# Value stages: an earlier first row sum, a block's weight split by halves, and the x transfers issued by ScalarE

## The chip, the cores and the metric

The kernel runs on one core of a Trainium2 chip. Times are device microseconds of one execution. A core has five engines that run their own instruction streams and wait for one another through semaphores: TensorE (PE) multiplies matrices, VectorE (DVE) and ScalarE (ACT) work elementwise on SBUF and PSUM, GpSimd (POOL) elementwise on SBUF, and SyncE (SP) issues transfers. ScalarE can issue transfers too.

## The reference

```python
def mixer_a(h, w_in, ln_g, ln_b, w_s, b_s, w_out):
    u, v, z = jnp.split(h @ w_in, 3, axis=-1)          # h: 2048 x 1024, w_in: 1024 x 6144
    u = jax.nn.gelu(u)
    v = layer_norm(jax.nn.gelu(v), ln_g, ln_b)
    ... # causal 128 x 128 mixing of v in each chunk of 128 positions, 8 channel groups
    y = u * mixed.reshape(B, S, A_WIDTH) * jax.nn.silu(z)
    return y @ w_out                                   # 2048 x 1024

# layer A
h = rms_norm(x, a_norm[i]) * (1.0 + scale) + shift
x = x + gate * mixer_a(h, ...)
# layer B: the shared k, v are projected from rms_norm(x, kv_norm); sliding-window attention
# over the same x, an output gate, an output projection; then one final rms_norm
```

All inputs are float32: x is 1 x 2048 x 1024.

## The kernel before, in words

**Token groups.** Layer A is worked through in four groups of 512 tokens (`NG = 4`, `i` = 0 to 3). A group has a value stage (v of `w_in`), eight steps for u and z with the spatial mixing, and the out projection with `w_out`. Layer B follows for all tokens.

**Precision by splitting.** Every product is three matmuls (`split3`, lines 2361 to 2363): each operand is a rounded part and a rest, hi x hi, hi x lo and lo x hi. For raw weights ScalarE rounds (`hi`, line 1364) and GpSimd subtracts to get the rest (`lo`, line 1130; for the out blocks (2,q) VectorE does, line 2116). Weight pieces come by halves: half of a unit is 512 KB raw. Some weight combinations are kept in DRAM already split ("kept": 1 MB for half of a unit) and need no rounding.

**Value stage, groups 1 to 3.** The product is done with seven block products instead of eight (a Strassen-like scheme), twice: `v_blocks(0)`, then `v_blocks(1)`. Units are numbered `v_unit(i, 0..13)`; unit n < 7 is block n of the first half. Blocks 0, 3 and 5 (units 0, 3, 5, 7, 10, 12) have raw weights, the others kept ones. Blocks 2, 4, 5 and 6 multiply sums of h (`s1` to `s4`), which GpSimd forms in the first value half (`s_sums`, `s_add`), ScalarE rounds (`s_round`) and GpSimd completes (`s_rest`, line 1176). They serve for both halves. The sum buffer `hfw` shares its place with `uu`, so VectorE waits for all eight sums of a group before it writes the third block's output.

**Out projection.** Again seven block products, (m, q) for product m and half q of the rows, in the order (0,0) (1,0) (0,1) (1,1) (2,0) (2,1) (3,0) (3,1) ... (6,1). The left operands `yb` are rounded by ScalarE (`factor_round`, line 1540) and completed by VectorE (`factor_rest`, line 2093). `out_keep(m)` (line 1547) copies a finished product out of PSUM on ScalarE. Meanwhile the next group's x is loaded (`load_x`), squared (`x_squares`), scaled (`x_scale`) and transposed during the last blocks.

**Order of transfers.** All weight loads are issued by SP in one hand-written order, each half when TensorE has freed its buffer. Between them stand the stores of x1 (group i-1's residual, `x1d`, line 993, after unit 9, four transfers of 512 KB) and `load_x(i + 1)` (line 928, one transfer of 2 MB, after out block (2,0)'s load). SP's transfers go on the queue that the profile calls q1, ScalarE's on q10.

Of the kernel before, what the change touches and what calls it, by code (L numbers as in the profile page):

```python
# [12 lines left out]
P = 128  # L13
# [4 lines left out]
T = 512  # L18
NG = SEQ // T
# [257 lines left out]
def combs_out(i, m):  # L277

    return 16 * sum(comb_stores(comb) for comb in COMBS if comb[0] <= i and comb[4] == m)
# [115 lines left out]
def yoco_kernel(nc, x, c, positions, a_norm, a_ada_w, a_ada_b, a_w_in, a_ln_g, a_ln_b, a_w_s, a_b_s,  # L395
# [3 lines left out]
    with ctx:  # L399
# [181 lines left out]
        def at(name, i, k):  # L581

            return per[name] * i + k
# [70 lines left out]
        def pieces(u, k):  # L654

            return PIECES_BY[u] + k
# [120 lines left out]
        def _(sp):  # L777
# [141 lines left out]
                    else:  # L919
                        b_half(u, hh)  # L920

            def load_x(n):
                if n >= 1:
                    sp.wait_ge(xt_full, at("xt_full", n - 1, 8))
                    sp.wait_ge(v_gelu, at("v_gelu", n - 1, 16))
                    sp.wait_ge(comb_out[0], combs_out(0, 0))
                    sp.wait_ge(piece_done, pieces(ao_block(n - 1, 1, 0), 4))
                sp.dma_start(xs[:], x[0, T * n:T * n + T, :].rearrange("(c p) d -> p c d", p=P)).then_inc(x_in, 16)

            def load_residual(i):  # L930
                if i == NG - 1:
                    sp.wait_ge(xt_full, at("xt_full", i, 8))
# [40 lines left out]

            for n in range(2 * KT):
                if n == 5:
                    load_x(0)
                load_ada(n)
            unit(0)
            unit(1)
# [1 line left out]
            for i in range(NG):  # L981
                if i == 0:
                    for j in range(4):
                        a_stage(0, j)
                else:
                    for n in range(2, V_UNITS[i]):
                        unit(v_unit(i, n))
                        if n == 11:
                            load_split(split_at(i, 3))
                        if n == 9:  # L990
                            sp.wait_ge(ao_read, at("ao_read", i - 1, 8))
                            for cnk in range(NC):
                                sp.dma_start(x1d[i - 1, :, cnk], x1[:, cnk, :]).then_inc(x1_out, 16)
                for g in range(GROUPS + 1):
                    a_stage(i, 4 + g)
                    if i >= 1 and g >= 2:
                        keep_turned(i - 1, g - 2)
                for n in range(2, 16):
                    if i == 0 and n == 15:
                        combs_kept(0)  # L1000
                    unit(ao_first(i) + n)
                    if i >= 1 and n == 4:
                        keep_turned(i - 1, GROUPS - 1)
                    if i < NG - 1 and n == 4:
                        load_x(i + 1)
                    if n == 7:
                        load_residual(i)
                    if i == NG - 1 and n in (6, 8, 10):
                        load_xk(0, n // 2 - 3)
                    if i == NG - 1 and n == 14:  # L1010

                        sp.wait_ge(piece_done, pieces(ao_block(i, 5, 1), 4))
                        sp.dma_start(hb0[:].bitcast(F32), hbd[0, 0:4].rearrange("k p a t -> p k a t")) \
                            .then_inc(hb0_in, 16)
# [78 lines left out]
        def _(pool):  # L1093
# [75 lines left out]
                pool.drain()  # L1169
                s_add(2, q, h_block(0, 1, q), ALU.subtract, s_whole(0, q))  # L1170

            def s_rest(i, s):
                for q in range(2):
                    there = S_ORDER[s][:, 2 * q:2 * q + 2]
                    pool.wait_ge(s_hi, s_parts(i, s, q))
                    g.tensor_tensor(there[:, :, 1, :], s_whole(s, q), there[:, :, 0, :].bitcast(F32),
                                    ALU.subtract).then_inc(s_lo, 1)
# [24 lines left out]
            for i in range(NG):  # L1202
# [5 lines left out]
                else:  # L1208

                    pool.wait_ge(piece_done, PIECES_BY[FIRST[i]])  # L1210
                    pool.wait_ge(xt_full, at("xt_full", i, 8))
                    s_sums(0)
                    pool.wait_ge(h_hi, at("h_hi", i, 8))
                    s_sums(1)
                    s_rest(i, 0)
                    for q in range(2):
                        s_add(3, q, h_block(0, 0, q), ALU.subtract, h_block(1, 0, q))
                    lo(v_unit(i, 3))
                    s_rest(i, 1)
                    s_rest(i, 2)  # L1220
                    lo(v_unit(i, 5))
# [128 lines left out]
        def _(act):  # L1350
# [46 lines left out]
            def load_positions(j):  # L1397
                act.dma_start(tabi[:], positions[:, T * j:T * j + T].broadcast_to([P, T])).then_inc(pos_in, 16)

            def squares(src, total, waste):  # L1400
                act.drain()
                return s_.activation(waste, src, ACT.Square, accum_out=total)
# [71 lines left out]
            for i in range(NG):  # L1474
# [20 lines left out]
                def v_blocks(sv):  # L1495
# [5 lines left out]
                        s_.activation(ut[:, c, :], bank(2 * sv + c), ACT.Copy).then_inc(first_kept, 1)  # L1501
                    if sv == 0:
                        s_round(i, 0, (1,))
                        s_round(i, 1)
                        s_round(i, 2)
                    hi(v_unit(i, 7 * sv + 3))
                    if sv == 0:
                        s_round(i, 3)
                    else:
                        x1_squares(i - 1)  # L1510
                    hi(v_unit(i, 7 * sv + 5))
                    for c in range(2):
# [88 lines left out]
                factor_round(2, 1)  # L1601
                hi(ao_block(i, 2, 1), (0,))
                out_keep(1)
                hi(ao_block(i, 2, 1), (1,))
                for q in range(2):
                    factor_round(3, q)
# [1172 lines left out]
```

## Time and profile before

| | |
|---|---|
| median of 3 runs | 2218.93 us (2217.34 to 2219.06) |
| profiled execution | 2219.44 us |
| its span, first to last instruction | 2217.7 us |
| mean granted TensorE clock | 0.996 |
| TensorE matmuls busy | 2150.9 us, 97% |
| VectorE, ScalarE, GpSimd busy | 65%, 49%, 54% |

The span is what the trace covers; the difference to the execution's own time lies outside the instructions. The granted clock is TensorE's clock as a share of full speed. In the rows below, a time in brackets is how long the engine sat idle before the instruction and what it waited for; "xN" merges N like instructions. A matmul's own duration of 0.39 us overlaps its neighbours'.

### The profile page before, as it was taken

The numbers are of one execution on the slowest core, as the hardware profiler recorded it, in microseconds if no ns is written. First come the engines' busy times: TensorE is split into PE (matmuls) and PEld (weight loads), VectorE is DVE, ScalarE is ACT, GpSimd is POOL, SyncE is SP. The second block draws the span as 40 slices with busy tenths as digits, with TensorE's granted clock in tenths as the row PEclk, the third lists the DMA queues.
The fourth block names the chain that finished last, engine by engine and source line by source line (L and its number), as shares of the span: only waits on it lengthen the run. The fifth ranks groups of instructions, "written<-read, shape, count | busy, mean of one in ns | idle before, by whom it ended". The sixth has DMA issues, their size and how long they took to land.

```text
span 2217.7 us, 29383 instructions
## 1 busy us (share of the span) xinstructions
PE 2150.9 (97%) x10410; PEld 1801.0 (81%) x10410; DVE 1440.5 (65%) x1761; ACT 1095.3 (49%) x2050; POOL 1195.1 (54%) x913
## 2 busy tenths in 40 slices
PE   5999999999999999999999999999999999999998
PEld 4887778788888878888777888887888888888887
DVE  6956548757486864554974673767767657656854
ACT  4334446634545744445653445534545646545653
POOL 3456675845553865544594645441535555454542
PEclk9999999999999999999999999999999999999999
DMA  9888889785558785557877556899686697887654
GB/s 347 307 306 308 312 315 356 231 308 174 196 198 324 285 315 191 200 179 269 314 259 283 181 181 218 323 348 365 244 297 225 253 359 266 280 309 288 206 205 171
DMA packets 244787, 592.89 MB, mean 267 GB/s; under 512 B 20929, under 2 KB 96801, under 8 KB 244257
## 3 DMA queue, kind: packets, MB, share of 16 engines
q1 hardware_dynamic: 241680, 585.71, 73.5%
q10 hardware_dynamic: 2960, 5.30, 0.7%
q8 instruction: 83, 1.36, 0.2%
q14 instruction: 64, 0.52, 0.1%
HBM read 461.96 MB, written 119.54 MB: 262 GB/s over the span
## 4 chain that ended last, share of the span: by engine, by line
PE 75%; DMA 6%; POOL 6%; DVE 5%; ACT 3%; DVEq 2%; POOLq 1%; issue 1%; SPq 1%; ACTq 0%
PE ps L2361 22%; PE ps L2363 22%; PE ps L2362 22%; DMA w_raw<-in_a_w_in 3%; POOL w_lo L1130 3%; PE ps L2566 2%; PE ps L2615 1%; PE ps L2616 1%; POOL cbl L1149 1%; PE ps L2641 1%; DVE acc L1812 1%; ACT w_hi L1364 1%; DMA w_lo<-a_weights_combined 1%; PE ps L2650 1%; DVE yb L2093 1%
## 5 line engine op out<-in xcount | busy, mean ns | idle before, releaser
L1130 POOL TENSOR_TENSOR w_lo<-w_raw,w_hi 128x1024 fp32r<-128x1024 f32 x244 | 650.0, 2682 | 569.6 <-ACT w_hi L1364 569.4
L1364 ACT ACTIVATE w_hi<-w_raw 128x1024 fp32r<-128x1024 f32 x260 | 272.0, 1057 | 418.3 <-DMA w_raw<-in_a_w_in 372.7
L2361 PE MATMUL ps<-h,w_hi 128*128 128x512 f32 x1024 | 403.3, 394 | 9.7 <-POOL w_lo L1130 8.3
L2363 PE MATMUL ps<-h,w_lo 128*128 128x512 f32 x1024 | 398.9, 390 | 0.0
L2362 PE MATMUL ps<-h,w_hi 128*128 128x512 f32 x1024 | 398.7, 389 | 0.0
L2361 PEld LDWEIGHTS ps<-h,w_hi 128*128 128x128 f32 x1024 | 192.2, 188 | 55.3 <-POOL w_lo L1130 14.3
L2363 PEld LDWEIGHTS ps<-h,w_lo 128*128 128x128 f32 x1024 | 192.2, 188 | 40.7
L2362 PEld LDWEIGHTS ps<-h,w_hi 128*128 128x128 f32 x1024 | 192.4, 188 | 38.9 <-issue 0.2
L2361 PE MATMUL ps<-r,w_hi 128*128 128x512 f32 x480 | 191.6, 399 | 1.9 <-issue 1.9
L2363 PE MATMUL ps<-r,w_lo 128*128 128x512 f32 x480 | 187.7, 391 | 0.0
L2362 PE MATMUL ps<-r,w_hi 128*128 128x512 f32 x480 | 187.3, 390 | 0.0
L2361 PE MATMUL ps<-w_hi,yb 128*128 128x512 f32 x448 | 179.2, 400 | 7.1 <-DVE w_lo L2116 3.5
L2071 DVE SCALAR_TENSOR_TENSOR wz<-wz,ps 128x512 f32<-128x512 f32 x64 | 43.7, 686 | 210.5 <-ACT wz L1580 210.5
L2363 PE MATMUL ps<-w_hi,yb 128*128 128x512 f32 x448 | 175.8, 392 | 0.0
L2362 PE MATMUL ps<-w_lo,yb 128*128 128x512 f32 x448 | 175.6, 392 | 0.0
L2093 DVE TENSOR_TENSOR yb<-vy,yb 128x1024 fp32r<-128x1024 f32 x48 | 114.4, 2383 | 42.5 <-ACT yb L1540 39.2
L1269 POOL TENSOR_SCALAR_AFFINE_SELECT p_edge<-pt 64x256 fp32r<-64x256 f32 x64 | 27.1, 423 | 187.7 <-ACT pt L1735 186.5
L2361 PE MATMUL ps<-w_hi,r 128*128 128x512 f32 (+1 forms) x352 | 125.5, 357 | 2.7 <-DMA r<-kv_input 1.7
L1735 ACT ACTIVATE pt<-ps 128x512 fp32r<-128x512 f32 x64 | 38.4, 600 | 179.6 <-PE ps L2641 179.2
L2363 PE MATMUL ps<-w_hi,r 128*128 128x512 f32 (+1 forms) x352 | 123.6, 351 | 0.0
L2362 PE MATMUL ps<-w_lo,r 128*128 128x512 f32 (+1 forms) x352 | 123.5, 351 | 0.0
L2361 PE MATMUL ps<-w_hi,h 128*128 128x512 f32 x272 | 107.9, 397 | 4.5 <-POOL w_lo L1130 4.2
(277 smaller groups left out, 4902.6 us busy)
## 6 DMA issues: line engine op xcount, KB each, us to landing
w_raw<-in_a_w_in SPq DMA_DIRECT2D x256, 256.0 KB, 3.6
w_hi<-b_weights_split SPq DMA_DIRECT2D x104, 512.0 KB, 4.7
w_lo<-b_weights_split SPq DMA_DIRECT2D x104, 512.0 KB, 6.3
w_raw<-in_a_w_in SPq DMA_DIRECT2D x52, 512.0 KB, 4.7
w_raw<-in_a_w_out SPq DMA_DIRECT2D x48, 512.0 KB, 5.4
w_hi<-v_weights_combined SPq DMA_DIRECT2D x48, 512.0 KB, 3.9
w_lo<-v_weights_combined SPq DMA_DIRECT2D x48, 512.0 KB, 5.2
w_hi<-a_weights_combined SPq DMA_DIRECT2D x32, 512.0 KB, 6.6
```

Of the source, the lines that this page charges most:

```text
L1130: g.tensor_tensor(wlo[p][:, rows_], raw[p][:, rows_], whi[p][:, rows_].bitcast(F32), ALU.subtract).then_inc(w_lo, 1)
L1149: last = g.tensor_tensor(cbl[m][:, rows_], cbr[m][:, rows_], cbh[m][:, rows_].bitcast(F32), ALU.subtract)
L1269: return g.affine_select(out=heads, in_=in_, compare_op=ALU.is_ge, fill=0.0, base=0, pattern=[[0, 4], [1, HEAD]], channel_multiplier=-1)
L1364: s_.activation(whi[p][:, rows_], raw[p][:, rows_], ACT.Copy).then_inc(w_hi, 1)
L1735: s_.activation(pt[:, 0, :], bank(6), ACT.Copy).then_inc(pt_hi, 1)
L1812: v.scalar_tensor_tensor(there, rows_, sc[:, kt:kt + 1], there, ALU.mult, ALU.add).then_inc(ada_used, 1)
L2071: v.scalar_tensor_tensor(wz[:, ft, :], wz[:, ft, :], 1.0, bank(2 + ft), ALU.add, ALU.mult) \
L2093: v.tensor_tensor(there[:, :, 1, :], y_factor(m, q), there[:, :, 0, :].bitcast(F32), ALU.subtract) \
L2361: t_.matmul(dst_, stat[0], mov[0], start=start, stop=False)
L2362: t_.matmul(dst_, stat[0], mov[1], start=False, stop=False)
L2363: return t_.matmul(dst_, stat[1], mov[0], start=False, stop=stop)
L2566: last = t_.matmul(bank(4 + ft, P, P * cnk), vs[:, cnk, P * ft:P * ft + P], wst[:, g, :], start=True, stop=True)
```

## The change

Four edits. In GpSimd's stream the first row sum's rest for the first half is moved ahead of the second half's sums, and the fourth block's (unit 3's) weight rests are split around the two sums of the fourth kind. In ScalarE's stream the rounding of unit 3 is split around the second sum's rounding. The stores of x1 move from SP (after unit 9) to ScalarE (after unit 10's rounding, ahead of `x1_squares`). The loads of x for groups 1 to 3 move from SP to ScalarE, behind `out_keep(1)`; the load for group 0 stays with SP.

```diff
@@ block.sync
-            def load_x(n):
-                if n >= 1:
-                    sp.wait_ge(xt_full, at("xt_full", n - 1, 8))
-                    sp.wait_ge(v_gelu, at("v_gelu", n - 1, 16))
-                    sp.wait_ge(comb_out[0], combs_out(0, 0))
-                    sp.wait_ge(piece_done, pieces(ao_block(n - 1, 1, 0), 4))
-                sp.dma_start(xs[:], x[0, T * n:T * n + T, :].rearrange("(c p) d -> p c d", p=P)).then_inc(x_in, 16)
...
                 if n == 5:
-                    load_x(0)
+                    sp.dma_start(xs[:], x[0, 0:T, :].rearrange("(c p) d -> p c d", p=P)).then_inc(x_in, 16)
...
                         if n == 11:
                             load_split(split_at(i, 3))
-                        if n == 9:
-                            sp.wait_ge(ao_read, at("ao_read", i - 1, 8))
-                            for cnk in range(NC):
-                                sp.dma_start(x1d[i - 1, :, cnk], x1[:, cnk, :]).then_inc(x1_out, 16)
...
-                    if i < NG - 1 and n == 4:
-                        load_x(i + 1)
@@ block.gpsimd
-            def s_rest(i, s):
-                for q in range(2):
+            def s_rest(i, s, halves=(0, 1)):
+                for q in halves:
...
                     s_sums(0)
+                    s_rest(i, 0, (0,))
                     pool.wait_ge(h_hi, at("h_hi", i, 8))
                     s_sums(1)
-                    s_rest(i, 0)
+                    s_rest(i, 0, (1,))
+                    lo(v_unit(i, 3), (0,))
                     for q in range(2):
                         s_add(3, q, h_block(0, 0, q), ALU.subtract, h_block(1, 0, q))
-                    lo(v_unit(i, 3))
+                    lo(v_unit(i, 3), (1,))
                     s_rest(i, 1)
@@ block.scalar
+            def load_x(n):
+                act.wait_ge(xt_full, at("xt_full", n - 1, 8))
+                act.wait_ge(v_gelu, at("v_gelu", n - 1, 16))
+                act.wait_ge(comb_out[0], combs_out(0, 0))
+                act.wait_ge(piece_done, pieces(ao_block(n - 1, 1, 0), 4))
+                act.dma_start(xs[:], x[0, T * n:T * n + T, :].rearrange("(c p) d -> p c d", p=P)).then_inc(x_in, 16)
...
                     if sv == 0:
                         s_round(i, 0, (1,))
+                        hi(v_unit(i, 3), (0,))
                         s_round(i, 1)
+                        hi(v_unit(i, 3), (1,))
                         s_round(i, 2)
-                    hi(v_unit(i, 7 * sv + 3))
-                    if sv == 0:
                         s_round(i, 3)
                     else:
+                        hi(v_unit(i, 10))
+                        act.wait_ge(ao_read, at("ao_read", i - 1, 8))
+                        for cnk in range(NC):
+                            act.dma_start(x1d[i - 1, :, cnk], x1[:, cnk, :]).then_inc(x1_out, 16)
                         x1_squares(i - 1)
...
                 out_keep(1)
+                if i < NG - 1:
+                    load_x(i + 1)
                 hi(ao_block(i, 2, 1), (1,))
```

## Rows read from the trace of the kernel before

**Rows 1.** The page's list: busy time (share of the span) x instructions.

```profile
PE 2150.9 (97%) x10410; PEld 1801.0 (81%) x10410; DVE 1440.5 (65%) x1761; ACT 1095.3 (49%) x2050; POOL 1195.1 (54%) x913
```

**Rows 2.** TensorE in order of time, first value half, group 1: start, duration, instruction.

```profile
430.28 0.39 PE L2362 MATMUL ps<-w_lo,h 128*128 128x512 f32 x1
430.51 0.39 PE L2363 MATMUL ps<-w_hi,h 128*128 128x512 f32 x1
431.58 0.47 PE L2361 MATMUL ps<-w_hi,s 128*128 128x512 f32 x1 [0.68 <-issue]
...
437.65 0.50 PE L2361 MATMUL ps<-w_hi,h 128*128 128x512 f32 x1 [0.38 <-POOL w_lo L1130]
...
440.52 0.39 PE L2361 MATMUL ps<-w_hi,h 128*128 128x512 f32 x1
```

**Rows 3.** TensorE in order of time, unit 10 in groups 1, 2, 3.

```profile
477.33 0.50 PE L2361 MATMUL ps<-w_hi,h 128*128 128x512 f32 x1 [1.28 <-POOL w_lo L1130]
...
830.63 0.50 PE L2361 MATMUL ps<-w_hi,h 128*128 128x512 f32 x1 [0.84 <-POOL w_lo L1130]
...
1186.73 0.50 PE L2361 MATMUL ps<-w_hi,h 128*128 128x512 f32 x1 [0.95 <-POOL w_lo L1130]
```

**Rows 4.** TensorE in order of time, out block (2,1) of group 2.

```profile
1074.98 0.76 PE L2361 MATMUL ps<-w_hi,yb 128*128 128x512 f32 x1 [2.10 <-DVE w_lo L2116]
...
1078.43 0.39 PE L2363 MATMUL ps<-w_hi,yb 128*128 128x512 f32 x1
```

**Rows 5.** Windows view, that stretch: length, engines' busy time, PEclk, DMA share, GB/s.

```profile
1074.00:1080.00 6.00, 5.02 (x15) 4.08 (x16) 5.82 (x4) 6.00 (x7) 3.53 (x2) 0.72 0.99 365
```

**Rows 6.** GpSimd in order of time, first value half, group 1.

```profile
426.05 1.29 POOL L1159 TENSOR_TENSOR s1f<-hfw 128x512 f32<-128x512 f32 x1
...
430.19 2.54 POOL L1176 TENSOR_TENSOR s<-s2f,s 128x512 fp32r<-128x512 f32 x2
432.69 2.55 POOL L1159 TENSOR_TENSOR s3f<-hfw 128x512 f32<-128x512 f32 x2
435.19 4.78 POOL L1130 TENSOR_TENSOR w_lo<-w_raw,w_hi 128x1024 fp32r<-128x1024 f32 x2
```

**Rows 7.** SP in order of time, second value half, group 1.

```profile
460.60 2.86 SPq L993 DMA_DIRECT2D x_kept<-x  x4
463.50 2.62 SPq L807 DMA_DIRECT2D w_raw<-in_a_w_in  x2
```

**Rows 8.** ScalarE in order of time, unit 10's rounding, group 1.

```profile
473.76 1.06 ACT L1364 ACTIVATE w_hi<-w_raw 128x1024 fp32r<-128x1024 f32 x1 [7.96 <-DMA w_raw<-in_a_w_in]
```

**Rows 9.** SP in order of time, out projection, group 2.

```profile
1057.42 0.63 SPq L928 DMA_DIRECT2D xs<-in_x  x1
1059.32 3.04 SPq L797 DMA_DIRECT2D w_raw<-a_weights_combined  x2
```

**Rows 10.** ScalarE in order of time, out block (2,1), group 2.

```profile
1070.58 1.06 ACT L1364 ACTIVATE w_hi<-w_raw 128x1024 fp32r<-128x1024 f32 x1 [2.73 <-DMA w_raw<-a_weights_combined]
```

**Rows 11.** VectorE in order of time, the same place.

```profile
1072.23 1.47 DVE L1917 TENSOR_TENSOR up<-up,ps 128x512 f32<-128x512 f32 x2 [1.58 <-ACT uq L1547]
1073.62 2.35 DVE L2116 TENSOR_TENSOR w_lo<-w_raw,w_hi 128x1024 fp32r<-128x1024 f32 x2
```

**Rows 12.** Queues from 698 to 699 us: packets, MB, share of 16 engines.

```profile
q10 hardware_dynamic: 56, 0.22, 52.9%
q1 hardware_dynamic: 72, 0.16, 44.3%
```

**Rows 13.** SP in order of time, out blocks (3,0) and (3,1), group 1.

```profile
710.79 8.53 SPq L801 DMA_DIRECT2D w_raw<-in_a_w_out  x4
```

**Rows 14.** ScalarE in order of time, second half of block (3,1), group 1.

```profile
723.75 1.06 ACT L1364 ACTIVATE w_hi<-w_raw 128x1024 fp32r<-128x1024 f32 x1 [1.01 <-DMA w_raw<-in_a_w_out]
```

**Rows 15.** VectorE in order of time, rests of the fifth block's factor, group 1.

```profile
725.80 2.92 DVE L2093 TENSOR_TENSOR yb<-vy,yb 128x1024 fp32r<-128x1024 f32 x1 [0.43 <-ACT yb L1540]
...
731.92 2.50 DVE L2093 TENSOR_TENSOR yb<-vy,yb 128x1024 fp32r<-128x1024 f32 x1
```

**Rows 16.** TensorE in order of time, out block (5,1), group 1.

```profile
756.11 0.50 PE L2361 MATMUL ps<-w_hi,yb 128*128 128x512 f32 x1 [0.22 <-POOL w_lo L1130]
```

## Prediction

> **What bounds the kernel now.** I read the page's list of engines first: TensorE's matmuls fill 2150.9 of 2217.7 us [rows 1]. So an edit is worth what it gives back of TensorE's remaining pauses, or costs in new ones, and everything else waits behind it. Next came TensorE's rows in order of time, looking only at rows with an idle time in brackets. In a stretch without pauses matmuls start 0.227 us apart (430.28, 430.51) [rows 2]. At the pause behind them the step is 1.07, so 0.84 is lost where the bracket says 0.68: a loss is the bracket plus 0.16. From 437.65, behind a pause, twelve matmuls take 2.87 where twelve steps are 2.73, so about 0.14 more goes in restarting. I price a pause at its bracket plus 0.3. A unit of 24 matmuls is 5.46 us, its half 2.73.
>
> The pauses that the edits can reach are of three kinds; the first two come once in each of the token groups 1 to 3:
> - first value half: before the third and the fourth block, 0.68 and 0.38 [rows 2]; the other two groups repeat it to within 0.03;
> - second value half: before its fourth block (unit 10), 1.28, 0.84 and 0.95 [rows 3];
> - out projection of group 2: 2.10 before block (2,1), after which eight steps take 3.45 us instead of 1.82 [rows 4]; the granted clock of that stretch is 0.72, a mix of 2.4 and 1.2 GHz [rows 5].
>
> **First value half: the row sums.** The third block needs GpSimd's rest of the first row sum. Now both halves' sums are made first, the second from 426.05 to 430.19 (4.14 us), then the two rests (2.54), two sums of the fourth kind (2.55) and the fourth block's two weight rests (4.78) [rows 6]. With the first rest moved ahead: it runs 426.05 to 427.3, the sums to 431.5, the other rest to 432.7, the fourth block's first weight half to 435.1, the two sums to 437.6, the second weight half to 440.0. TensorE would begin the third block at 430.74 (no pause), want its second half at 433.5 (there since 432.7), begin the fourth at 436.2 (there since 435.1), and want that block's second half at 438.9. That is there at 440.0, because GpSimd has done the same work by then in either order. So the pause moves: this half began at 440.52 [rows 2] and will begin at about 440.05, plus the restart. Worth 0.4 us a group, 1.2 in three. Bounds: 0, if GpSimd runs 0.4 slower in the new order; 5.0 if both pauses went whole (0.98 + 0.68 with restarts, three times). I take 1.2, since every duration in it is from a row.
>
> ScalarE's reordered roundings (the fourth block's split among them) run about 1 us ahead of GpSimd and cost nothing. VectorE waits for all eight sums before the third block's output; those now end 2.5 us later, at 437.6 instead of 435.2. It takes up slack that VectorE has by the fifth block, so I price it at nothing; without that cover it would hold the banks of the fifth block and cost up to 1 us.
>
> **Second value half: the x stores.** SP issues four 512 KB stores of x1 at 460.60, takes 2.86 us over them, and only then issues unit 10's weights at 463.50 [rows 7]. ScalarE is free for them, waits 7.96 us and starts at 473.76 [rows 8]: 10.3 us from issue to use. Then GpSimd takes 2.4 and TensorE has paused. After the change SP issues that load when TensorE frees its buffer, eight halves after 440.52, at 462.3 (near 462 with the first pauses shorter). The 2 MB of stores are gone from ahead of it, 5.7 us at the 365 GB/s of a full stretch [rows 5], which leaves 4.6 of the 10.3, say 6. So ScalarE rounds near 468.5 and GpSimd is done by 472, where TensorE wants it at 475.9. The stores are issued by ScalarE when it has dispatched unit 10's rounding, near 471, and are under way until 479, beside units 11 and 12. Unit 12 is wanted at 486.8, two units later. The wait for `ao_read` holds nothing: the squares behind it wait for the same. ScalarE's issuing of four stores (2.9 us, SP's own time) lies in the wait that is gone. I count all three pauses: (1.28 + 0.84 + 0.95) + 3 x 0.3 = 4.0 us. Bounds: 0 and 4.0.
>
> The Trainium skill (DMA: Bandwidth & Descriptors, Rules for kernel authors) says that spreading transfers over SP and ScalarE brings no bandwidth, because all run on the same engines, and saves only issue time. By it this edit would give only what the stores' later place gives; were they in flight with unit 10 all the same, the 4.0 would be near 0.
>
> **Out projection: the x load, its gain.** In group 2, SP issues the 2 MB x load at 1057.42 and block (2,1)'s first half at 1059.32 behind it [rows 9]. ScalarE gets it at 1070.58, after a wait of 2.73 [rows 10], so its copy of `uq` and with it VectorE are late (a wait of 1.58); VectorE then adds for 1.4 us and needs half of 2.35 for the first weight rest [rows 11]. Without the wait VectorE starts its additions at 1070.7, has that rest at 1073.4, and TensorE, which wants it at 1072.7, pauses 0.5. Now the step costs 2.26 + 1.63 = 3.9 [rows 4]; after, 0.8, at full clock. Gain 3.1.
>
> **Out projection: the x load, its cost.** ScalarE issues it behind the copy of `uq`, two units (11 us) later than SP did. Where the two queues were both loaded, in one microsecond 56 packets of q10 (ScalarE's) and 72 of q1 (SP's) moved [rows 12]: about one for one. The x load is 512 packets of 4 KB (a row of 1024 floats); at 64 a microsecond it is under way for 8 us, and lands some 10 us after its issue, before the squares need it. But in these 8 us SP fetches block (3,1), packets of 2 KB (512 floats), 256 to a half: each half takes 4 us instead of 2. In group 1 the last of them is issued near 719 [rows 13] and ScalarE waits for it until 723.75 [rows 14]; I put it 2.3 later, at 726.0. The rounding behind it is what VectorE waits for at 725.80 [rows 15], and from there VectorE is busy without a gap up to the factors of block (5,1), where TensorE pauses 0.22 already [rows 16]. VectorE gets some back: its step of 2.50 at 731.92 [rows 15] runs beside GpSimd, and moved behind GpSimd's work takes 1.23 as half of 2.35 did [rows 11]. So 2.3 becomes 1.0 in group 1; the same reckoning gives 0.6 in group 0 and 1.0 in group 2. ScalarE and GpSimd also start block 3's rests 0.4 to 0.9 sooner, worth 0.3 in groups 0 and 1. In all: 3.1 - 1.0 - 1.0 - 0.6 + 0.6, say +0.8 (in group 2 I leave 0.3 for the small pauses that its big one covered). Bounds: +3.7 if VectorE feels nothing, -3.6 if it gets nothing back (3.1 less 1.9, 2.3 and 2.5).
>
> The Trainium skill (DMA: Bandwidth & Descriptors, Queues, rings and completion order) has each engine take turns between rings, packet by packet. By that rule 4 KB packets get twice the bytes of 2 KB ones, as reckoned, and the trace agrees (56 against 72).
>
> **Sum.** 1.2 + 4.0 + 0.8 = 6.0 us. The profiled execution took 2219.4 (1.7 of it outside its span, which no edit touches), which gives 2213.4; it stands 0.5 above the median of the three runs, 2218.93, so I predict 2212.9, 0.27% faster. A measurement of this kernel tells about 0.2%, 4.4 us.
>
> **The rivals.**
> - *The x load is free (or frees more).* VectorE's 2.3 us vanish in its overlap with GpSimd: sum 1.2 + 4.0 + 3.1 = 8.3, 2210.6. For it: VectorE's operations shrink from 2.5 to 1.2 beside an idle GpSimd. Against: no gap on VectorE in 30 us. 0.25.
> - *VectorE gives nothing back.* Out projection -3.6: sum 1.6, 2217.3, no change that can be measured. 0.15.
> - *A second queue is no second road.* By the skill's rule above, as a mechanism here: the stores, moved by ScalarE, still meet unit 10 and then units 11 and 12, and TensorE's pause moves to one of these. Gain of the stores' edit 0: 6.0 - 4.0 = 2.0, 2216.9. Against: unit 12 is wanted 7 us after the stores end. 0.1.
> - *Slower: the late x load throttles the clock.* TensorE's pause at block (5,1) reaches 2 us, as the one in group 2 did [rows 4], and the granted clock falls, 1.6 more each time. It decides from a delay of about 2 us on VectorE that isn't given back. In three groups: 1.9 + 2.3 + 2.5 and 3 x 1.6 = 11.5 lost, against 1.2 + 4.0 + 3.1 = 8.3: 3.2 slower, 2222.1. 0.1.
> - The row sums do nothing (their pause moves whole): 1.2 less, inside the forecast.
>
> **How the numbers follow.** Forecast 0.4, its own range 2211 to 2215.5; the free load 0.25, nothing back 0.15, no second road 0.1, slower 0.1. One thing is common to all: a clock that falls elsewhere by chance, 1.6 either way. From 2208.5 to 2219.0 lies all but the slow case and the far end of the free one, 8 in 10. Faster by over 0.2% means below 2214.5: all of the free case and 0.9 of the forecast, 0.62; slower 0.1; the rest, 0.28, within.
>
> **What would show it.** Right: no pause before unit 10; third block at its step, a pause of about 0.9 in the middle of the fourth; in group 2 a pause below 1 at (2,1) and clock 1.0; ScalarE's wait for block (3,1) in group 1 ending 2 us later, relative to TensorE, and a pause near 1.2 at (5,1). Wrong: a pause at units 11 to 13 or in the fifth block of the first half; a granted clock below 1 in groups 0 to 2; the x load landing more than 12 us after its issue.

## The result, and the profile after

The changed kernel takes 2223.78 us (median of 16 runs, 2220.62 to 2230.14); the kernel before takes 2218.64 beside it (16 runs, 2216.03 to 2221.58). The ratio is 1.0027, with a 95% interval of 1.0020 to 1.0034. That is 6.0 us slower (4.4 to 7.5; the two medians are 5.1 apart), where I had forecast 6.0 faster. The time lies outside my range, and on the side to which I gave 0.1. The profiled execution of the changed kernel was its slowest run, 2230.14 us, span 2228.3, so its trace shows more loss than a usual run. A second profile of the same kernel (c1 below, 2218.77 us) tells which of it returns.

From the page of the changed kernel, its list of engines (for [rows 1]):

```profile
PE 2153.1 (97%) x10410; PEld 1801.6 (81%) x10410; DVE 1448.6 (65%) x1761; ACT 1095.8 (49%) x2050; POOL 1184.5 (53%) x913
```

TensorE still sets the time, so the difference has to lie in its pauses. Its rows in order of time (start, duration, instruction, idle time and releaser), pauses only; the first three lie in the value stage of group 1 and answer to [rows 2, 3], the other three in the out projections of groups 1 and 2, the fifth of them in the place of [rows 4]:

```profile
442.14 0.50 PE L2362 MATMUL ps<-w_hi,h 128*128 128x512 f32 x1 [1.01 <-POOL w_lo L1116]
...
462.44 0.47 PE L2362 MATMUL ps<-w_hi,h 128*128 128x512 f32 x1 [0.95 <-DVE vy L1975]
...
490.44 0.50 PE L2362 MATMUL ps<-w_hi,s 128*128 128x512 f32 x1 [0.56 <-POOL w_lo L1116]
...
753.07 0.50 PE L2362 MATMUL ps<-w_hi,yb 128*128 128x512 f32 x1 [3.27 <-DVE yb L2094]
...
1081.19 0.47 PE L2362 MATMUL ps<-w_hi,yb 128*128 128x512 f32 x1 [0.60 <-DVE w_lo L2117]
...
1112.02 0.50 PE L2362 MATMUL ps<-w_hi,yb 128*128 128x512 f32 x1 [2.64 <-DVE yb L2094]
```

The first is the pause that I had moved to the middle of the fourth block. The second is new: the first block of the second value half waits for VectorE. The third stands before unit 12 (its operand is `s`), while unit 10 pauses no more; in groups 2 and 3 unit 12 pauses 0.75 and 1.72. The one of 0.60 stands before block (2,1) of group 2, where the kernel before had 2.10. The pauses of 3.27 and 2.64 stand before block (5,0). Behind the one at 753 the granted clock falls to 0.72, a mix of 1.2 and 2.4 GHz. The table of windows shows it (columns: the stretch, its length, then busy time and count of TensorE's matmuls, its weight loads, VectorE, ScalarE and GpSimd, then granted clock, DMA share, GB/s):

```profile
755.00:760.00 5.00, 5.00 (x17) 3.91 (x17) 4.82 (x3) 1.13 (x2) 5.00 (x3) 0.72 0.26 57
```

For all comparisons I cut each trace into stages by the starts of TensorE's first matmul in each stage. The table gives their durations in us. "Va" and "Vb" are the first and the second value half, each up to the next unit's start, in groups 1, 2, 3; "out" is the out projection of groups 0, 1, 2. The names are those of the experiments below:

| kernel | out 0 / 1 / 2 | Va 1 / 2 / 3 | Vb 1 / 2 / 3 |
|---|---|---|---|
| before | 81.31 / 82.08 / 84.08 | 39.82 / 39.81 / 39.83 | 39.66 / 39.23 / 39.33 |
| before, again (c2) | 81.29 / 82.51 / 82.79 | 39.80 / 39.82 / 40.59 | 40.16 / 38.89 / 38.21 |
| after | 82.59 / 86.24 / 86.06 | 40.63 / 40.60 / 40.60 | 39.31 / 39.21 / 40.21 |
| after, again (c1) | 82.72 / 82.86 / 82.64 | 39.46 / 40.59 / 39.45 | 39.17 / 39.86 / 38.93 |
| e1, sums only | 81.20 / 82.10 / 81.94 | 39.46 / 39.49 / 39.45 | 40.19 / 39.47 / 39.00 |
| e4, sums and two drains | 81.25 / 82.10 / 82.11 | 39.45 / 39.46 / 39.50 | 39.79 / 40.07 / 38.79 |
| e2, stores only | 81.28 / 82.08 / 82.11 | 39.81 / 39.81 / 40.59 | 39.68 / 41.46 / 39.67 |
| e3, load only | 82.85 / 84.36 / 82.62 | 39.80 / 40.57 / 39.80 | 39.64 / 38.17 / 39.12 |
| e7, load late on SP | 84.37 / 84.86 / 85.55 | 40.61 / 40.57 / 39.81 | 38.23 / 38.97 / 38.85 |
| e8, sums, stores on SP last | 81.46 / 82.17 / 82.08 | 40.57 / 40.59 / 40.60 | 39.33 / 39.69 / 40.26 |
| e9, stores late on SP | 81.34 / 82.08 / 82.17 | 40.59 / 39.79 / 39.80 | 42.51 / 41.65 / 42.27 |
| e10, stores split | 81.18 / 83.26 / 82.32 | 40.61 / 39.80 / 39.81 | 38.20 / 38.08 / 38.08 |
| e11, stores early | 81.44 / 81.97 / 81.84 | 39.81 / 40.28 / 40.27 | 38.08 / 38.17 / 38.20 |
| e12, e11 with sums | 81.36 / 82.08 / 82.30 | 40.60 / 40.60 / 40.63 | 38.20 / 38.18 / 38.20 |

A second value half without a pause is seven units, 7 x 5.46 = 38.2.

### The profile page after: what moved, and what is told of

Same layout as the page of the kernel before. It is cut to its first block, busy times and chain, and to the rows that moved or that the text cites. A ratio compares the mean times of both kernels' runs of the same rounds, so it can differ in the third digit from the quotient of the medians.

```text
span 2228.3 us, 29383 instructions
## 1 busy us (share of the span) xinstructions
PE 2153.1 (97%) x10410; PEld 1801.6 (81%) x10410; DVE 1448.6 (65%) x1761; ACT 1095.8 (49%) x2050; POOL 1184.5 (53%) x913
## 4 chain that ended last, share of the span: by engine, by line
PE 74%; DMA 6%; DVE 6%; POOL 6%; ACT 3%; DVEq 2%; POOLq 1%; issue 1%; SPq 1%; ACTq 0%
PE ps L2362 22%; PE ps L2364 22%; PE ps L2363 22%; DMA w_raw<-in_a_w_in 3%; POOL w_lo L1116 3%; PE ps L2567 2%; PE ps L2616 1%; PE ps L2617 1%; POOL cbl L1135 1%; PE ps L2642 1%; ACT w_hi L1352 1%; DVE acc L1813 1%; DVE yb L2094 1%; DMA w_raw<-in_a_w_out 1%; PE ps L2651 1%
## 5 line engine op out<-in xcount | busy, mean ns | idle before, releaser
L2362 PE MATMUL ps<-h,w_hi 128*128 128x512 f32 x1024 | 403.3, 394 | 10.1 <-POOL w_lo L1116 8.4
```

What stands on the lines that cost most here:

```text
L2362: t_.matmul(dst_, stat[0], mov[0], start=start, stop=False)
```

## The experiments

e1, e2, e3, e7, e9, e10 and e11 are the kernel before with one edit; e4, e8 and e12 have one more on top of e1's; c1 and c2 are the changed kernel and the kernel before once more. Each was timed beside the kernel before (median 2217.37 beside e1 to e4, 2217.25 beside e7, e8, e9 and c1, 2216.94 beside e10, e11, e12 and c2), in 11 or 12 runs, e7 and e9 in 5.

### The three edits, one by one

**e1: the row sums alone.**

```diff
                     s_sums(0)
+                    s_rest(i, 0, (0,))
                     pool.wait_ge(h_hi, at("h_hi", i, 8))
                     s_sums(1)
-                    s_rest(i, 0)
+                    s_rest(i, 0, (1,))
+                    lo(v_unit(i, 3), (0,))
                     for q in range(2):
                         s_add(3, q, h_block(0, 0, q), ALU.subtract, h_block(1, 0, q))
-                    lo(v_unit(i, 3))
+                    lo(v_unit(i, 3), (1,))
```

with ScalarE's roundings in the matching order.

> Only the order of the row sums, their rests and the fourth block's roundings in the first value half is changed; stores and x load stay on SP. Theory 'starved': in the changed kernel VectorE waits for all eight sums, its next 128x512 operation then starts inside an unbroken run of GpSimd and takes 8.09 us instead of 1.77, and TensorE pauses 0.95 at the first block of the second value half, three times: 3 x (0.95 + 0.3) = 3.75 lost against the 1.2 that I forecast as gain, so about 2.5 slower than before (2221.2), with the 8.09 and the 0.95 in its trace in all three groups. Rival 'sums are harmless' (the 8.09 comes from the queues' other order): 1.2 faster, 2217.4, and the operation near 1.8.

Measured: 2216.95 us, ratio 1.0000 (0.9991 to 1.0008). The operation took 0.89 us in group 1 and no long one stood in any group; the pause of 0.95 was absent. In its trace the first halves gain 0.36 us each, 1.1 in three, as forecast (1.2). The time itself can't show it: 1.1 lies within its interval of 2 us either way.

**e4: the same with gaps in GpSimd's stream.**

```diff
                     lo(v_unit(i, 5))
+                    pool.drain()
                     s_rest(i, 3)
+                    pool.drain()
                     lo(v_unit(i, 7))
```

> The row sums' order as in the changed kernel, and GpSimd drains before the rest of the fourth row sum and before unit 7's rest, which opens small gaps in its stream; nothing else is changed. Theory 'starved': a gap lets VectorE's operation through, it takes 2 to 4 us instead of 8, the pause of 0.95 goes, and the time is 2 to 3 below the kernel with the sums alone. Rival: the gaps are too short, the operation stays at 8.09 and the time at that of the sums alone; then only the operation's start, not GpSimd's breath, matters.

Measured: 2216.48 us, ratio 0.9997 (0.9988 to 1.0006), no long operation. Since e1 had none either, the gaps had nothing to cure: inconclusive.

**e2: the stores alone.**

```diff
-                        if n == 9:
-                            sp.wait_ge(ao_read, at("ao_read", i - 1, 8))
-                            for cnk in range(NC):
-                                sp.dma_start(x1d[i - 1, :, cnk], x1[:, cnk, :]).then_inc(x1_out, 16)
...
                     else:
+                        act.wait_ge(ao_read, at("ao_read", i - 1, 8))
+                        for cnk in range(NC):
+                            act.dma_start(x1d[i - 1, :, cnk], x1[:, cnk, :]).then_inc(x1_out, 16)
                         x1_squares(i - 1)
```

Unit 10's rounding stands just ahead of these lines, so ScalarE's order is that of the changed kernel.

> Only the stores of x1 move, from SP ahead of unit 10 to ScalarE behind unit 10's rounding. Theory of the prediction: the three pauses at unit 10 go, 4.0 faster (2214.6). Rival 'no second road' (the changed kernel's trace has 0.56, 0.54 and 1.72 before unit 12 where unit 10 had 1.28, 0.84 and 0.95): the pause moves to unit 12 and stays about as large, 0 to 1 faster (2217.6 to 2218.6).

Measured: 2221.02 us, ratio 1.0023 (1.0013 to 1.0033), slower. No pause at unit 10; before unit 12 the pauses are 1.31, 2.21 and 1.19. The rival's place is right, and even its 0 to 1 faster was too kind. The profile is of e2's slowest run, 2226.04 us.

**e3: the x load alone.**

```diff
-                    if i < NG - 1 and n == 4:
-                        load_x(i + 1)
...
                 out_keep(1)
+                if i < NG - 1:
+                    load_x(i + 1)
```

with `load_x` written for ScalarE as in the changed kernel.

> Only the x load moves, from SP to ScalarE behind the copy of uq. Theory 'late beside block (3,1)': the load takes the transfers' time from block (3,1), VectorE is late, and TensorE pauses 3.3 at (5,0) in group 1 and 2.6 in group 2 with the clock falling (1.6 each), against the 3.1 gained at (2,1) in group 2: some 4 slower than before (2222 to 2223). Rival of the prediction: 0.8 faster (2217.8), with pauses near 1.2 at block 5; then the large pauses of the changed kernel come from VectorE's phase that the other two edits set.

Measured: 2220.34 us, ratio 1.0017 (1.0009 to 1.0026), slower by 2 to 6. Its largest pauses in the out projections are 1.44 in group 0, 1.59 in group 1 (at 750.28) and 0.71 in group 2, all at (5,0) and near the 1.2 that I had forecast at block 5. The total is not near it, because there was next to no gain at (2,1) to set against them. The clock did not fall there.

### The same kernels once more

> The changed kernel once more, for a second profile. If its large pauses at (5,0) (3.27 and 2.64 us) and VectorE's operation of 8.09 us belong to it, they are there again in the same groups; if they are chance, groups 1 and 2 of the out projection take 84 and 82.6 us as with the x load alone moved, and 8.09 turns up in some groups only. Time 2220 to 2224.

Measured: 2222.41 us, ratio 1.0023 (1.0014 to 1.0032). The pauses at (5,0) are 1.33, 0.70 and 0.70, the clock stays at 1.00 behind them, and the long operation is there in group 2 alone. So 3.27 and 2.64 with the fallen clock belong to one execution, not to each.

> The kernel before once more, for a second profile. If the pause of 2.10 us at block (2,1) of group 2, on which I put a gain of 3.1, belongs to the x load's place, it is there again and the third out projection takes 84 us; if it was chance (no trace of the kernels that leave the x load on SP has it), it takes 82.1 and the pause is 0.6 to 0.9. Time 2217 to 2218, ratio 1.000.

Measured: 2217.75 us, ratio 1.0007 (0.9997 to 1.0017). At block (2,1) of group 2 the second profile of the kernel before and that of e1, which leaves the load where it was, have, in TensorE's rows:

```profile
1074.98 0.47 PE L2361 MATMUL ps<-w_hi,yb 128*128 128x512 f32 x1 [1.54 <-DVE w_lo L2116]
```

```profile
1075.16 0.47 PE L2364 MATMUL ps<-w_hi,yb 128*128 128x512 f32 x1 [0.69 <-DVE w_lo L2119]
```

Over the ten traces with the load in its old place this pause is 2.10, 1.54, 1.05, 1.04, 0.92, 0.83, 0.83, 0.78, 0.69 and 0.60, and the clock falls behind it in the first alone. With the load on ScalarE it is 0.59 to 0.60 in all three. Group 1 scatters in the same way: 0.71 to 0.97 in nine of the ten and 2.01 in the tenth (e10), there without a fall of the clock, against 0.78 to 0.81 with the load on ScalarE.

### Time or queue?

**e9: the stores late, on SP** (`if n == 9` becomes `if n == 11`, ahead of unit 12's load).

> The stores of x1 stay on SP but are issued late, ahead of unit 12's load, at the time when the changed kernel's ScalarE issues them; nothing else is changed. Theory 'the place in time costs, not the queue': the transfers have their hole before 472 and are full until 492, unit 12 is late by as much as with the stores on ScalarE or more (it stands behind all 2 MB), 2219 to 2222. Rival 'the second queue costs' (SP's issues beside ScalarE's took 1.2 to 1.6 us instead of 0.43 to 0.47): without it the pause at unit 12 is under 0.5, 2214 to 2216.

Measured: 2226.42 us, ratio 1.0047 (1.0033 to 1.0060), more than the 2219 to 2222 that I had expected. The pause stands at unit 12: 2.44, 2.37, 2.28, and the second halves carry 8.8 us of the loss. Late on SP's queue costs more than late on ScalarE's; there unit 12's load stands behind all 2 MB. So it isn't ScalarE's queue that costs: the late place costs on either.

**e7: the x load late, on SP** (`n == 4` becomes `n == 7`, behind block (3,1)).

> The x load stays on SP but is issued late, behind the loads of block (3,1) and ahead of the residual's load; nothing else is changed. Theory 'a hole in the transfers' (they are busy without a break from before the stage to about 740 in the kernel before; with the x load on ScalarE their busy share falls to 0.75 and 0.45 between 708 and 716 and they then stay full until 744): the hole is the same here, the queue is not, so the out projections lose about what they lose with the load on ScalarE (1.6, 2.3, 0.6 us against 81.25, 82.1 and 82.1), at (3,1) or behind it, some 2220 to 2222. Rival 'sharing with block (3,1)': that block's loads are not held up now, ScalarE waits for them no longer than before, and the kernel is at 2217.

Measured: 2226.72 us, ratio 1.0045 (1.0033 to 1.0058); the three out projections take 3.1, 2.6 and 3.2 us more than on average with the load in its old place. I had expected 2220 to 2222. The rival, that the loss comes from sharing with block (3,1) alone, is out: that block now goes first, and the loss is larger. That the sharing adds its part where there is some, in e3 and the changed kernel, is not excluded.

The table of windows shows what is common to both. For the out projection of group 1, first the second profile of the kernel before, then e3, then e7 (the last two columns are the DMA engines' busy share and GB/s):

```profile
708.00:716.00 8.00, 8.00 (x36) 6.31 (x35) 7.72 (x5) 2.10 (x4) 3.01 (x1) 1.00 1.01 397
...
736.00:744.00 8.00, 8.00 (x37) 6.63 (x36) 7.32 (x9) 7.05 (x7) 1.38 (x1) 1.00 0.82 307
```

```profile
708.00:716.00 8.00, 8.00 (x37) 6.61 (x36) 7.72 (x6) 2.73 (x5) 2.88 (x1) 1.00 0.60 200
...
736.00:744.00 8.00, 8.00 (x38) 6.60 (x36) 7.39 (x8) 6.40 (x8) 3.05 (x2) 1.00 1.03 408
```

```profile
716.00:724.00 8.00, 8.00 (x37) 6.64 (x36) 7.45 (x8) 4.95 (x7) 0.00 (x0) 1.00 0.59 188
...
744.00:756.00 12.00, 10.16 (x45) 8.07 (x43) 9.43 (x11) 8.80 (x9) 2.62 (x2) 1.00 1.02 397
```

With the load in its old place the transfers are full when the load goes and slacken at 736. Moved, it leaves a hole of 0.60, because SP's next loads wait for buffers that TensorE has not freed (in e3 SP issues nothing from 709.9 to 712.3), and its 2 MB then lie on top of a stretch that is full anyway and now stays full to 744 (e3) or 756 (e7).

### Where the stores can go

For the second value half of group 1, the windows of the second profile of the kernel before, and of the changed kernel:

```profile
464.00:472.00 8.00, 8.00 (x37) 6.64 (x36) 2.42 (x4) 0.63 (x2) 0.00 (x0) 1.00 1.03 385
472.00:484.00 12.00, 10.43 (x47) 8.30 (x46) 3.94 (x6) 7.78 (x11) 5.97 (x4) 1.00 1.04 392
484.00:488.00 4.00, 4.00 (x20) 3.30 (x19) 0.69 (x1) 2.10 (x3) 3.98 (x2) 1.00 0.75 292
488.00:496.00 8.00, 8.00 (x37) 6.64 (x36) 3.26 (x5) 0.29 (x1) 0.79 (x1) 1.00 0.33 87
```

```profile
464.00:472.00 8.00, 8.00 (x37) 6.64 (x36) 6.77 (x11) 4.39 (x7) 0.78 (x1) 1.00 0.69 214
472.00:484.00 12.00, 12.00 (x54) 9.94 (x54) 4.63 (x7) 5.67 (x9) 5.24 (x4) 1.00 0.99 373
484.00:488.00 4.00, 4.00 (x19) 3.30 (x19) 0.69 (x1) 1.06 (x1) 0.02 (x1) 1.00 1.07 395
488.00:496.00 8.00, 7.44 (x33) 5.82 (x32) 3.26 (x5) 2.10 (x3) 4.75 (x2) 1.00 0.68 256
```

The hole is at 464 to 472 (0.69 for 1.03, 8 x 0.34 = 2.7 us of transfer time), and the full stretch ends behind 488 where it ended before 488. The changed kernel's second half starts 3.3 us later in its trace (462.44 for 459.15), but that isn't the hole: its share from 465.3 to 473.3 is 0.65, and that of the kernel before from 462 to 470, as far behind its own start, is 1.02. Other places for the stores tell whether the hole is the cause.

**e8: on SP, behind the last value unit's loads** (`n == 13`), with the sums' order.

> The row sums' order as in the changed kernel; the stores of x1 stay on SP but are issued behind the loads of the last value unit, near 485, where the transfers of the kernel before run dry (busy share 0.03 at 488 to 492); the x load as before. Theory 'a hole in the transfers': unit 10's load no longer has 2 MB ahead of it and unit 12's none beside it, so both pauses go: 3 to 4 faster than the sums' order alone, 2213 to 2214. Rival 'second value half is bound by other things': the pause turns up elsewhere in the half, and it stays at 2217.

Measured: 2217.74 us, ratio 1.0000 (0.9991 to 1.0009), where I had expected 2213 to 2214. Units 10 and 12 pause no more, but the first of the gate's units does: 0.97, 1.35 and 1.90. The rival was right. The hole is the same, as its window shows:

```profile
464.00:472.00 8.00, 8.00 (x37) 6.61 (x36) 6.99 (x12) 4.40 (x8) 0.50 (x1) 1.00 0.67 215
```

**e10: split,** two stores ahead of unit 10's load, two behind the last value unit's.

```diff
-                        if n == 9:
+                        for cnk in {9: (0, 1), 13: (2, 3)}.get(n, ()):
                             sp.wait_ge(ao_read, at("ao_read", i - 1, 8))
-                            for cnk in range(NC):
-                                sp.dma_start(x1d[i - 1, :, cnk], x1[:, cnk, :]).then_inc(x1_out, 16)
+                            sp.dma_start(x1d[i - 1, :, cnk], x1[:, cnk, :]).then_inc(x1_out, 16)
```

> Kernel before, with the four stores of x1 split on SP: two ahead of unit 10's load as before, two behind the loads of the last value unit. Theory 'a hole in the transfers': with 1 MB ahead of it unit 10's load has little left to lose, 1 MB fills the hole that opened at 464 to 472 when all four were moved, and the other 1 MB falls where transfers run dry (488 to 492): the pauses at unit 10 (about 1.0 each) shrink below 0.4, none comes at unit 12 or the gate's units, 2 to 4 faster, 2213 to 2215. Rival 'whatever is moved comes back later': pause at the units behind, 2217.

**e11: each store as soon as its chunk is complete.** Chunks 0 and 1 of x1 are complete before the first value half ends.

```diff
-                        if n == 9:
-                            sp.wait_ge(ao_read, at("ao_read", i - 1, 8))
-                            for cnk in range(NC):
-                                sp.dma_start(x1d[i - 1, :, cnk], x1[:, cnk, :]).then_inc(x1_out, 16)
+                        for cnk in {7: (0, 1), 8: (2,), 9: (3,)}.get(n, ()):
+                            sp.wait_ge(ao_read, at("ao_read", i - 1, 5 + cnk))
+                            sp.dma_start(x1d[i - 1, :, cnk], x1[:, cnk, :]).then_inc(x1_out, 16)
```

> Kernel before, with each store of x1 issued on SP as soon as its chunk is complete: chunks 0 and 1 behind unit 7's loads (near 449, where the transfers' busy share is 0.66 to 0.85), chunk 2 behind unit 8's, chunk 3 behind unit 9's. Theory 'a hole in the transfers': 1 to 1.5 MB go into time in which the transfers were partly idle, nothing is postponed, and unit 10's load has 0.5 MB ahead of it instead of 2: its pauses fall below 0.3 and none comes behind, 3 to 4 faster, 2213 to 2214.5. Rival 'the first half's weights need that time': a pause at unit 7, 8 or 9, no gain, 2217 to 2219.

**e12: e11 with the sums' order.**

> The early stores together with the row sums' order of the changed kernel. If the two add, 0.4 a group on top of the early stores alone (1.1 in all), unless VectorE's operation is starved (8.09 us, 1.15 lost each time it happens): 2212 to 2215.

Measured: e10 2216.60 us, ratio 0.9996 (0.9986 to 1.0007); e11 2215.67 us, 0.9997 (0.9989 to 1.0006); e12 2216.65 us, 0.9998 (0.9989 to 1.0006). All three miss the ranges that I had expected. The windows of e10, then of e11:

```profile
464.00:472.00 8.00, 8.00 (x37) 6.63 (x36) 5.79 (x10) 4.97 (x8) 0.86 (x1) 1.00 0.96 331
```

```profile
464.00:472.00 8.00, 8.00 (x37) 6.61 (x36) 3.67 (x7) 2.43 (x4) 0.00 (x0) 1.00 1.03 411
```

The hole is filled, and in all nine second halves of these three kernels there is no pause at a unit (38.1 to 38.2 us, the bare 38.2). That bears out the hole as the cause of the later pauses, in the traces of the halves. The times do not add to it: they gain less than the 3 us that the halves show, and none differs from the kernel before by more than its interval. Part is given back: in e11 the first halves of groups 2 and 3 take 0.47 more each (VectorE's long operation, 5.4 us there), in e12 each first half has the long operation, and in e10 one has it and the out projection of group 1 pauses 2.01. The rest is within the interval of 2 us. No kernel here is shown to beat the kernel before.

## Why the prediction was wrong, step by step

**The sum.** It now reads, by means over all traces of the table: sums +0.1, stores +1.5, load +5.1 (its gain at (2,1) taken off), together 6.7 us slower; 6.0 was measured. I had -1.2, -4.0 and -0.8. How the loss divides between stores and load is less sure than that it is theirs: timed one by one, the three edits cost 0.0, 5.1 and 3.8 us, each to about 2 us, 8.9 when added.

**Row sums: order right, size right, and nothing gained.** GpSimd did what I wrote, to within 0.1 us once the 2.1 that this trace runs later are taken off (its rows in the changed kernel, for [rows 6]; TensorE's pause is the 1.01 above):

```profile
428.14 1.28 POOL L1162 TENSOR_TENSOR s<-s2f,s 128x512 fp32r<-128x512 f32 x1
...
433.53 1.31 POOL L1162 TENSOR_TENSOR s<-s2f,s 128x512 fp32r<-128x512 f32 x1
434.79 2.42 POOL L1116 TENSOR_TENSOR w_lo<-w_raw,w_hi 128x1024 fp32r<-128x1024 f32 x1
...
439.68 2.41 POOL L1116 TENSOR_TENSOR w_lo<-w_raw,w_hi 128x1024 fp32r<-128x1024 f32 x1
```

A half takes 39.46 for 39.81. What I had no price for is VectorE, which sometimes takes 8 us over one operation (last section); my "up to 1 us" was for a wait in the fifth block. Such a half takes 40.60, 1.14 more; in the old order 40.59, 0.78 more. It happened in 10 of 18 halves with the new order and in 7 of 21 with the old (e11 left out), so the means are 40.10 and 40.07: nothing. Whether the new order makes it likelier, these counts don't settle; the 8-sum wait as its cause is not shown, since e1 and e4 have that wait and not the operation.

**Stores: the failed step is "the 2 MB of stores are gone from ahead of it", taken as a gain with no debt.** Unit 10's load came as expected (ScalarE rounds it 4.7 us after its issue instead of 10.3), and its pause went. But I asked of the stores' new place only whether unit 12 "is wanted 7 us after the stores end". That reckoned with the stores alone. The same full stretch also had to bring unit 11's kept weights, a split load and unit 12's own 1 MB. SP's rows of the changed kernel (for [rows 7]), then ScalarE's:

```profile
465.43 3.10 SPq L807 DMA_DIRECT2D w_raw<-in_a_w_in  x2
...
473.95 1.61 SPq L794 DMA_DIRECT2D w_lo<-v_weights_combined  x1
475.61 1.26 SPq L836 DMA_DIRECT2D wsr<-in_b_w_in  x1
476.91 1.62 SPq L838 DMA_DIRECT2D wsr<-in_b_w_in  x1
478.58 2.63 SPq L807 DMA_DIRECT2D w_raw<-in_a_w_in  x2
```

```profile
472.61 3.38 ACTq L1508 DMA_DIRECT2D x_kept<-x  x4
...
486.84 1.06 ACT L1352 ACTIVATE w_hi<-w_raw 128x1024 fp32r<-128x1024 f32 x1 [5.80 <-DMA w_raw<-in_a_w_in]
```

Unit 12 is issued at 478.58 and ScalarE rounds it 8 us later. In e8, with no stores beside it, the same load is issued 2.2 us sooner and rounded 5.1 us sooner (476.64 and 482.05, counted from the half's first matmul at 462.73 for 462.44). The 2.2 come from the three issues ahead of it, which took 1.3 to 1.6 us each instead of under 0.5 (last section); the rest is the load itself, 8.3 us from issue to rounding for 5.4. The second half then takes 39.72 on average (9 halves) for 39.21 with the stores in their old place (18 halves): 1.5 us lost in three groups. What was to be had was 39.21 - 38.2, 3.0 in three, for my 4.0. The rival "a second queue is no second road" named the mechanism, the pause that moves on to a later unit; I gave it 0.1 and let it end at a gain of nothing, because I didn't ask what the transfers would do in the time that the stores left. The Trainium skill's rule beside it (DMA: Bandwidth & Descriptors, Rules for kernel authors: a second queue brings no bandwidth) agrees with the windows above: from 472 to 484 us two queues moved 373 GB/s in the changed kernel, and one moved 392 in the kernel before. Of e2 one thing stays open: its ratio means 5.1 us (2.9 to 7.3), more than the mean 1.5 of the halves (3.2 in its own trace). Its trace shows 3 us more than the kernel before ahead of the first out projection, where nothing was edited and where these traces differ by 4 us among themselves (first matmul of that stage at 338.1 to 342.3). So the loss in time is shown, and its size by the halves is not.

**The x load's gain: the failed step is "gain 3.1".** It was read from one place of one trace, [rows 4], 2.26 and 1.63 behind it for the clock. The same trace has 0.80 at the same place in group 1 and nothing above 0.4 in group 0, which should have warned me. Over ten traces that pause averages 1.04, against 0.60 with the load moved: 0.4 gained.

**The x load's cost: mechanism partly right, size short.** I had 0.6, 1.0 and 1.0 for the three groups. The three traces with the load on ScalarE give 1.4, 2.2 and 1.4 over the means of the ten (81.31, 82.24, 82.37); the best of them, c1, gives 1.4, 0.6 and 0.3. The delay takes the way that I described, from block (3,1) through ScalarE to VectorE. ScalarE and VectorE in the changed kernel (for [rows 14, 15]; ScalarE's second line is the second half of block (3,1), as in [rows 14]):

```profile
728.94 1.06 ACT L1352 ACTIVATE w_hi<-w_raw 128x1024 fp32r<-128x1024 f32 x1 [2.99 <-DMA w_raw<-in_a_w_out]
730.46 1.07 ACT L1352 ACTIVATE w_hi<-w_raw 128x1024 fp32r<-128x1024 f32 x1 [0.46 <-DMA w_raw<-in_a_w_out]
```

```profile
732.51 3.42 DVE L2094 TENSOR_TENSOR yb<-vy,yb 128x1024 fp32r<-128x1024 f32 x1 [2.52 <-ACT yb L1539]
...
739.14 1.25 DVE L2094 TENSOR_TENSOR yb<-vy,yb 128x1024 fp32r<-128x1024 f32 x1
```

and the same places in its second profile:

```profile
724.35 1.06 ACT L1352 ACTIVATE w_hi<-w_raw 128x1024 fp32r<-128x1024 f32 x1 [3.10 <-DMA w_raw<-in_a_w_out]
725.71 1.06 ACT L1352 ACTIVATE w_hi<-w_raw 128x1024 fp32r<-128x1024 f32 x1 [0.30 <-DMA w_raw<-in_a_w_out]
```

```profile
721.32 9.95 DVE L2094 TENSOR_TENSOR yb<-vy,yb 128x1024 fp32r<-128x1024 f32 x3
```

The step of 2.50 came down to 1.25, given back as predicted. Counted from TensorE's first matmul of the stage (694.04, 691.94, and 691.42 in the kernel before), that half is rounded 36.4 us in, 33.8 in the second profile, and 32.3 in the kernel before. So the delay that I had put at 2.3 was 4.1 in the one and 1.4 in the other (3.8 in e3), though the x load was issued at the same place, 22.2 us in, in all three. In the second profile block (3,1) landed in time for VectorE to run on without a wait, and the pause was 0.70. In the first VectorE stood 2.52, and TensorE paused 3.27 and lost clock: my slower rival, one block earlier than written, in one execution of two. The delay sits at the edge of VectorE's slack, so a mean over its outcomes is worth more than the likeliest one.

A sign that I had named tells the cases apart, a load that lands more than 12 us after its issue. It landed after 12.9 and 12.6 us in groups 1 and 2 of the changed kernel and after 12.6 in group 1 of e3, with pauses of 3.27, 2.64 and 1.59 at (5,0). In the other groups 1 and 2 of the three traces it landed after 9.7 to 10.0, with pauses of 0.70 to 0.71. Group 0 does not follow this (9.9 to 10.1 us, with 0.71 to 1.44). Why the same load takes longer in one execution than in another is open.

**The chances.** The two largest terms rested on the assumption that bytes can be put off for nothing. The rivals varied them one at a time, and none had both fail. Range and chances were too sure for that. The slower rival's 2222.1 comes near the measured 2223.8 by luck: it put 8.4 net on the out projections, where the means over the traces show 5.1, and kept the gains of 4.0 and 1.2 in the value stages, which did not come. Two smaller slips changed nothing: the chance of a clear gain adds up to 0.61, not 0.62, and in [rows 12] ScalarE's queue moves 1.4 times the bytes of SP's (0.22 MB for 0.16), not twice.

## What to carry to other kernels

Before moving a transfer out of a stretch in which the DMA engines are full, ask what else could run in the time that it leaves. If the loads behind it wait for buffers, the time is lost, and the bytes come back on top of a later full stretch, by whichever queue. Move such transfers earlier, into a slack stretch, or leave part of them as filling; here that removed the pauses, though no gain in the whole time could be shown. A large pause that stands in one of several like places of a single trace can be chance, and needs a second trace before a forecast rests on it.

## What the runs showed of the hardware

**An operation that takes 0.9 us or 8.** It is VectorE's 128x512 product with both operands in SBUF, beside a stream of GpSimd. The changed kernel, VectorE, then GpSimd:

```profile
451.48 8.09 DVE L1905 TENSOR_TENSOR ur<-ur,gate_a 128x512 f32<-128x512 f32 x1
```

```profile
447.04 4.77 POOL L1116 TENSOR_TENSOR w_lo<-w_raw,w_hi 128x1024 fp32r<-128x1024 f32 x2
451.76 2.55 POOL L1162 TENSOR_TENSOR s<-s3f,s 128x512 fp32r<-128x512 f32 x2
454.26 4.76 POOL L1116 TENSOR_TENSOR w_lo<-w_raw,w_hi 128x1024 fp32r<-128x1024 f32 x2
```

and e1, where it starts as long before the end of GpSimd's operation (0.33 us):

```profile
450.65 0.89 DVE L1907 TENSOR_TENSOR ur<-ur,gate_a 128x512 f32<-128x512 f32 x1
```

```profile
446.24 4.74 POOL L1130 TENSOR_TENSOR w_lo<-w_raw,w_hi 128x1024 fp32r<-128x1024 f32 x2
450.95 3.44 POOL L1176 TENSOR_TENSOR s<-s3f,s 128x512 fp32r<-128x512 f32 x2
454.35 5.20 POOL L1130 TENSOR_TENSOR w_lo<-w_raw,w_hi 128x1024 fp32r<-128x1024 f32 x2
```

In the one case VectorE ends 0.55 us after GpSimd's stream does, and GpSimd is not slowed. In the other VectorE is through in 0.89, and it is GpSimd that takes longer (3.44 and 5.20 for 2.55 and 4.76). Long ones last 7.7 to 8.1 us, in 17 of the 42 first value halves of the table, and all others up to 3.1; only e11 has two of 5.4, which are its 0.47. What decides is not in the traces.

**Issues that take three times as long.** Beside and just behind ScalarE's four stores of 512 KB (issued from 472.61 to 475.99), SP's issues took 1.61, 1.26 and 1.62 us; in the kernel before the same three took 0.43, 0.43 and 0.47 (471.00 to 472.42). In eight of the nine places where ScalarE issues the stores some of SP's issues take over 1 us; in the ninth they take 0.67 and 0.87. But the last of the three began 0.9 us after ScalarE was done, and elsewhere single issues of SP take as long with no issue of ScalarE near (1.42 at 547.75 in the kernel before). So ScalarE's issuing goes with it and is not shown to be the cause.
